# Subtracting the rounded weights on GpSimd in pieces of 512 columns: a two-layer transformer step on one core

## What is computed

```python
for li in range(DEPTH):                                   # 2 layers
    m = silu(cond) @ w_mod + b_mod                        # (1024 x 6144): shifts, scales, gates
    h = rmsnorm(x, g_mix) * (1 + scale1) + shift1
    z = h @ w_in                                          # 1024 x 2720, split among four mixers
    # retention, windowed attention, differential attention, latent attention -> branches
    gates = sigmoid(h @ w_gate + b_gate)                  # 1024 x 4096
    x = x + gate1 * (sum(gates * branches @ w_branch) @ w_out)
    h2 = rmsnorm(x, g_ffn) * (1 + scale2) + shift2
    u = h2 @ w_up + b_up                                  # 1024 x 5632
    conv = b_conv + sum(w_conv[j] * shifted(u, j) for j in range(3))
    a, gg = split(conv)
    x = x + gate2 * ((silu(gg) * a) @ w_down)             # 2816 x 1024
```

## Time and profile before

| | us |
|---|---|
| median of 3 runs | 2620.35 |
| the runs | 2610.61, 2624.17, 2620.35 |
| the profiled execution, its own time | 2617.14 |
| its span | 2615.3 |
| PE busy | 2476.9 (95%) |
| DVE busy | 1310.0 (50%) |
| ACT busy | 878.0 (34%) |
| POOL busy | 607.2 (23%) |
| share of PE in the chain of work that ended last | 85% |
| share of DVE in that chain | 8% |

### The profile page before, as it was taken

One profiled execution on the slowest core, in us unless ns is written; L12 is line 12 of the kernel. 1 busy time (PEld: TensorE's weight loads), 2 busy tenths in 40 slices (PEclk: granted clock), 3 DMA queues, 4 the chain that ended last, 5 costly groups with the idle time before them and its releaser, 6 DMA issues.

```text
span 2615.3 us, 41235 instructions
## 1 busy us (share of the span) xinstructions
PE 2476.9 (95%) x16003; PEld 2250.8 (86%) x16003; DVE 1310.0 (50%) x2006; ACT 878.0 (34%) x1488; POOL 607.2 (23%) x139
## 2 busy tenths in 40 slices
PE   5999999989998999999969999999999989999998
PEld 3887787868898999999948877877789989999998
DVE  3333345633346773773842343365333567727557
ACT  3424334443223432322243242344432143313221
POOL 1211121101122333333213102111012223333331
PEclk7989999999999999999969899999999989999999
DMA  7412222122322222221272112321213222222211
GB/s 264 136 38 67 86 76 65 59 81 76 104 88 65 65 79 79 70 80 58 60 248 68 51 65 77 100 65 43 97 52 112 88 65 66 81 72 74 81 59 55
DMA packets 234461, 216.79 MB, mean 83 GB/s; under 512 B 8590, under 2 KB 217878, under 8 KB 234006
## 3 DMA queue, kind: packets, MB, share of 16 engines
q1 hardware_dynamic: 226614, 193.99, 23.5%
q10 hardware_dynamic: 7648, 20.09, 2.2%
HBM read 204.98 MB, written 9.08 MB: 82 GB/s over the span
## 4 chain that ended last, share of the span: by engine, by line
PE 85%; DVE 8%; issue 3%; ACT 3%; DMA 1%; DVEq 0%; ACTq 0%; SPq 0%
PE ps L682 53%; PE ps L738 11%; PE ps L767 4%; PE ps L829 3%; PE ps L802 3%; PE ps L817 2%; PE ps L693 2%; PE ps L1040 1%; DVE conv L1887 1%; DVE conv L1883 1%; PE ps L903 1%; PE ps L703 1%; DVE stat L1611 1%; ACT u_pad L1474 1%; DVE conv L1885 1%
## 5 line engine op out<-in xcount | busy, mean ns | idle before, releaser
L638 POOL TENSOR_TENSOR w_lo<-raw,w_hi 128x2048 fp32r<-128x2048 f32 (+2 forms) x132 | 606.8, 4598 | 1973.8 <-ACT w_hi L1183 1973.8
L682 PE MATMUL ps<-h_hi,w_hi 128*128 128x320 f32 x2432 | 633.8, 316 | 21.9 <-DVE gprod L1587 8.2
L682 PE MATMUL ps<-h_lo,w_hi 128*128 128x320 f32 x2432 | 621.1, 311 | 0.0
L682 PE MATMUL ps<-h_hi,w_lo 128*128 128x320 f32 x2432 | 620.8, 311 | 0.0
L682 PEld LDWEIGHTS ps<-h_hi,w_hi 128*128 128x128 f32 x2432 | 427.6, 190 | 34.5 <-DVE gprod L1587 8.2
L682 PEld LDWEIGHTS ps<-h_lo,w_hi 128*128 128x128 f32 x2432 | 426.9, 190 | 0.2
L682 PEld LDWEIGHTS ps<-h_hi,w_lo 128*128 128x128 f32 x2432 | 426.7, 190 | 0.0
L1183 ACT ACTIVATE w_hi<-raw 128x2048 fp32r<-128x2048 f32 (+2 forms) x132 | 245.6, 1861 | 314.9 <-PE ps L682 216.2
L1883 DVE TENSOR_SCALAR conv<-u_pad,vcol 128x642 f32<-128x642 f32 x88 | 222.1, 2524 | 116.5 <-ACT u_pad L1474 114.9
L1611 DVE TENSOR_REDUCE stat<-ps 128x1 f32<-128x640 f32 (+3 forms) x160 | 108.4, 678 | 264.7 <-PE ps L802 239.6
L738 PE MATMUL ps<-w_hi,h_hi 128*128 128x512 f32 (+1 forms) x480 | 184.2, 384 | 16.5 <-DVE h_lo L1558 15.4
(11 more groups left out here) (254 smaller groups left out, 3317.7 us busy)
## 6 DMA issues: line engine op xcount, KB each, us to landing
raw<-in_w_mod SPq DMA_DIRECT2D x48, 1024.0 KB, 5.2
raw<-in_w_up SPq DMA_DIRECT2D x88, 512.0 KB, 4.7
raw<-in_w_gate SPq DMA_DIRECT2D x32, 1024.0 KB, 5.6
raw<-in_w_in SPq DMA_DIRECT2D x20, 1024.0 KB, 5.1
raw<-in_w_down SPq DMA_DIRECT2D x16, 1024.0 KB, 5.0
w_br<-in_w_branch ACTq DMA_DIRECT2D x8, 1024.0 KB, 5.7
raw<-in_w_out SPq DMA_DIRECT2D x8, 1024.0 KB, 5.4
raw<-in_w_down SPq DMA_DIRECT2D x8, 768.0 KB, 4.8
```

The costliest lines, as they stand in the source:

```text
L638: nc.gpsimd.tensor_tensor(w_lo[s % WS][:, 0:n], raw[u % RAW][:, 0:n], w_hi[s % WS][:, 0:n].bitcast(F32), ALU.subtract).then_inc(lo_done.se ...
L682: ins = mm(out, w_at(w_hl[wi]), at_(x_hl[xi]), start=first and q == 0, stop=final and q == 2)
```

## The change

POOL's one subtraction of a unit becomes a row of subtractions of 512 columns each: four for a unit of 2048, three for 1536, two (512 and 128) for 640. Only the last one raises `lo_done`. Nothing else is changed.

```diff
@@ -635,8 +635,10 @@
                     n = unit_cols(u)
 
                     pool.wait_ge(hi_done.sem, now(hi_done, s + 1))
-                    nc.gpsimd.tensor_tensor(w_lo[s % WS][:, 0:n], raw[u % RAW][:, 0:n], w_hi[s % WS][:, 0:n].bitcast(F32),
-                                            ALU.subtract).then_inc(lo_done.sem, 1)
+                    for c0 in range(0, n, 512):
+                        c1 = min(n, c0 + 512)
+                        ins = nc.gpsimd.tensor_tensor(w_lo[s % WS][:, c0:c1], raw[u % RAW][:, c0:c1], w_hi[s % WS][:, c0:c1].bitcast(F32), ALU.subtract)
+                    ins.then_inc(lo_done.sem, 1)
                 pool.memset(token[:], 0.0).then_inc(raw_free.sem, 1)
```

## The result

| | before | after |
|---|---|---|
| median of the runs, us | 2622.26 (2610.12 to 2630.84, 6 runs) | 2594.53 (2585.82 to 2598.73, 6 runs) |
| the profiled execution, its own time | 2617.14 | 2593.88 |
| its span | 2615.3 | 2592.1 |
| mean granted clock of PE | 0.966 | 0.969 |
| PE busy | 2476.9 | 2472.2 |

The ratio is 0.9896, with a 95% interval of 0.9875 to 0.9917: 27.7 us between the medians, 23.3 us between the two profiled executions. The forecast was 18.2 us. PE is busy for 4.7 us less, so most of the gain lies in its idle gaps. The page's chain of the changed kernel breaks off early and gives 70% of the span to "issue" and 29% to POOL; it can't be read, and the gaps in PE's timeline take its place.

A forecast was written before the change was run, and what follows sets the result against it. PE, busy 95% of the span, was taken as the bound, so only its idle gaps count. Both layers' terms gave -15.0 us, the starts -3.7 and +0.45: -18.2, from 2620.35 to about 2602 us, range 2590 to 2615.

The forecast's parts named there:

- no turn: Rival: DVE gets no turn between pieces and stays out for 5.15 us instead of 4.6; slower, 2641 us; chance 0.08.
- Cost of a piece: POOL's subtraction: 1.29 us per 512 columns, 5.15 for four, a unit longer by 0.55; a boundary adds 0 to 0.18.
- Step 1: Start of layer 1: held scale row waits for one piece, so PE's 9.77 us gap shrinks; -3.7 us.
- step 2: Start of layer 0: `h_lo` comes behind the first unit instead of between two units; +0.45 us (0 to +0.7).
- Step 3: Start of the differential attention, both layers: PE's 2.04 us gap closes, -2.0 each; no clock fall behind it, -2.7 each.
- the clock doesn't come back: Rival: the low clock behind step 3's gap has other causes, so -2.7 is lost twice; 2607.5 us; chance 0.15.
- The last rival: More than forecast: clock fall behind the 461.76 gap, about 1 us, may be escaped; boundaries may be free; 2596; chance 0.11.
- Step 4: End of the differential attention, both layers: L1591 ends earlier, before PE's 2.85 us gap; -1.9 us each.
- Step 5: Windowed attention, both layers: gaps of 0.65 and 0.57 us behind a held L1638 close; -1.2 us each.
- Step 6: Behind the up tiles, both layers: PE's 1.38 us wait for the last `a_lo` shrinks; -0.5 us each.
- Step 7: Last group of down units, both layers: POOL ends 1.7 us later with 1.0 in hand; loss of +0.8 each.
- The MLP: POOL's work stays hidden behind PE; its starts go from 14.52 to 14.1 us apart, no `w_lo` wait in up tiles.

The follow-up runs named there:

- e9_start: Kernel before, with only the first two units of each layer cut into pieces of 512: 2614.98 us, ratio 0.9970 to the kernel before.
- e7_plan: Changed kernel, with pieces of 256 for units 17 to 22 and unit 64 whole: 2583.38 us, ratio 0.9854 to the kernel before.
- e2: Changed kernel, with pieces of 512 only for units 34 to 65 of each layer (MLP), others whole: 2628.03 us, ratio 1.0011 to the kernel before.
- e10: Changed kernel, with the first two units of each layer whole and all others in pieces of 512: 2596.72 us, ratio 0.9912 to the kernel before.
- e5_whole17: Changed kernel, with only unit 17 of each layer whole: 2604.46 us, ratio 0.9919 to the kernel before.
- e6_only17: Kernel before, with only unit 17 of each layer cut into pieces of 512: 2613.66 us, ratio 0.9965 to the kernel before.
- e4: Changed kernel, with pieces of 256 instead of 512: 2592.17 us, ratio 0.9889 to the kernel before.
- e8: Changed kernel, with POOL subtracting only the first 128 columns of each unit after units 0 and 1, whole there: 2580.53 us, ratio 0.9837 to before.
- e1_mixers: Changed kernel, with pieces of 512 only for units 0 to 33 of each layer, others whole: 2594.27 us, ratio 0.9892 to the kernel before.
- e11_scl_first: Kernel before, whole units, with POOL waiting for the scale row before each layer's first unit: 2616.55 us, ratio 0.9986 to the kernel before.

## Why the prediction was right, and where it was off

The decisive step, that DVE gets its turn at each boundary between two of POOL's instructions, held. It came from one row. The Trainium skill (GPSIMD Engine Reference, section Instruction dispatch) has it that consecutive instructions are no barrier between POOL's cores. It doesn't say what becomes of DVE's turn; that there might be none was the prediction's own conclusion. The rows at 846 to 851 show a turn at three boundaries of one unit; the measurement decides, and the rival "no turn" falls with it: no DVE instruction L1885 lasts longer than 1.48 us.

By the prediction's steps:

- **Cost of a piece.** 1.29 us each was right (median 1302 ns, with held ones in it), but four don't add up to 5.15, as they overlap a little: a unit with nothing inside lasts 4.96 (at 258.36), where it lasted 4.61. A boundary adds 0.12 us; the bounds were 0 and 0.18. The span of a unit with three DVE instructions inside was to grow by 2.2 us; it grew by 1.85 (5.12 to 6.97).
- **Step 1, start of layer 1: the size was right, the mechanism wrong.** The gap shrank by 3.66 us (3.7 forecast). But the step said that the scale row, held behind POOL, would wait for one piece. In the profile after it was first and waited for nothing, so that the size came out was luck. Where the row does lose to a piece (e9_start, and e7_plan in layer 1) the gap is 5.73, so the step's own path is worth 4.04. The forecast treated one draw of a race as fixed; it also took step 2's draw as fixed. It also had the clock the wrong way round: behind the first `h_lo` it stays low for a shorter time after (3.5 us in layer 0, 4.2 in layer 1) than before (5.5 and 6.0), not a longer one, which gave back 0.9 and 0.8 us.
- **Step 2, start of layer 0.** 5.62 to 6.09, the +0.45 forecast, in this pair of executions, where the row won both times. Where it loses, whole units cost 9.78 (e2, e10) and pieces 5.73 (e9), so that +0.45 turns into about -4. This draw is missing from the sum. e9_start, with only the first two units cut, is 6.7 us under the kernel before, where steps 1 and 2 add up to 3.25, but its interval holds both; the price comes from the gaps, not from this time. e10_rest, everything but those, is 25.0 under it. The two don't add up to the 27.7 exactly, but their intervals reach some 6 and 8 us to either side.
- **Step 3, the gap and the clock.** Both as forecast, -2.04 and no fall of the clock behind it, in both layers, and shown by putting back unit 17. Apart from the gap and the 0.40 named below, the executions part by 2.6 us between 391.7 and 426.6, for 2.7 forecast. The rival "the clock doesn't come back" falls at this place, since e5_whole17 and e6_only17 bring the low clock back and take it away. Not foreseen: the low stretch behind the gap at 453.2 lasts 6.8 us in this execution, not 3.4, and gives back 1.5 us a layer. The last rival had this clock recover instead; only e4, e7 and e8, where the gap itself is 0.57 us or less, have no fall there.
- **Step 4.** 2.85 to 0.83: -2.02 for a forecast of -1.9.
- **Step 5.** The gaps of 0.65 and 0.57 closed; e9_start, with whole units there, has 0.66 and 0.57. -1.2 as forecast.
- **Step 6.** 1.38 to 0.69: -0.69 for -0.5.
- **Step 7, the loss.** PE waits 0.43 us for `w_lo`, for 0.8 forecast. The mechanism is the named one: e1_mixers, whole there, has none, and e4_256, with more boundaries, has 1.01 and 2.16.
- **Given nothing.** The gap at 461.76 lost 0.24 us, as chains of three gain little; two gaps of 0.40 and 0.30 us behind held DVE instructions, at 426.6 and 627.0 in the profile before, closed in each layer and were not in the sum.
- **The MLP** stays hidden: POOL's starts lie 14.08 us apart (845.68, then 859.76) for 14.1 forecast, and PE waits for no `w_lo` in the up tiles.

The sum for the two profiled executions, PE's gaps and the clock behind them, from the terms above: a layer gives -2.04 - 2.7 - 2.02 - 1.22 - 0.69 + 0.43 - 0.24 - 0.70 + 1.5 = -7.7, twice -15.4, and the starts -3.66 + 0.47 = -3.2: 18.6 us. PE's waits for loads of w_mod are 1.8 us shorter in the execution after (5.9 for 7.7 in the view of PE's waits), which no step of the change accounts for. Of the other 2.9 us, 1.7 are the shorter low clock behind the first `h_lo` of the two layers; 1.2 are left unassigned. So 18.2 was the right size for this pair's gaps, and 5 us too low for the whole of it. The medians lie further apart, 27.7 us, and 18.2 lies outside of the interval (0.9875 to 0.9917, 22 to 33 us). Why isn't shown. The profiled execution of the kernel before is itself 5.1 us under its median, and the traces have two draws of that size that had fallen well for it and that the change makes cheap or removes: the race at the start of layer 0 (4.15 us, lost in two of the four traces) and the low clock behind the gap of 2.85 us (2.7 us, there at 4 of 10). How often the untraced runs lose either, no row says.

## What to carry to other kernels

Where GpSimd and VectorE met on operands in SBUF here, VectorE's wait was set by the length of GpSimd's single instruction: up to 4.82 us for L1883 behind whole units, 1.48 behind pieces. So look for a short VectorE instruction on the way to PE and cut GpSimd's there, and leave it whole where PE waits for GpSimd's own result. The cut cost GpSimd 0.12 us a boundary, and in addition the time of each instruction that got in (a unit of 5.12 us became one of 6.97 with three of them). Before a gap in one profile is priced, look whether two engines are issued within a few tenths of a microsecond there: then the row is one draw of a race, and the other draw belongs in the sum.

## What the runs showed of the hardware that wasn't expected

- A race that is lost by 0.19 us costs 4.15 us of PE's time at a layer's start (a gap of 9.77 against 5.62 in the kernel before), and with pieces it costs next to nothing (5.73 in e9_start). Adding a wait to win it lost the next one: `h_lo` held for 4.68 us in e11_scl_first.
- The same gap is followed by a low clock of 3.4, 6.8 or once 10.2 us in different executions. A fall followed every gap of 1.93 to 2.29 us before a transpose of the differential attention, none followed those of 0.83 (changed kernel) and 0.56 (e7_plan); yet behind the longer gap of 2.85 us it came at only 4 of 10 places.
- The runs of the kernel before lie 20.7 us apart among six, those of the changed kernel 12.9 among six, those of e7_plan 6.3 among five. Most of the scatter goes with the granted clock. In the 23 runs of the kernel before beside e9 to e11 the fastest (2606.71 us) has a mean of 0.971 and the slowest (2633.44) one of 0.961, and the product of a run's span and its clock varies by 6 us where the span varies by 27. The traces show two sorts of draws behind it, where low stretches fall and how long they last, and who wins a race while the clock is low; their shares weren't measured.
